# Four stages of a two-block transformer kernel: head loads, conv output, filler products in the routing, and the first expert's buffer given back in parts

## The chip, the core and the metric

The kernel runs on one core of one Trainium2 chip. The metric is the device time of one execution in microseconds (us). Engines are named as in the profile: PE (TensorE), with PEld for its weight loads, DVE (VectorE), ACT (ScalarE), POOL (GpSimd) and SP (SyncE). ACTq and SPq are the queues of ACT and SP at the place where they issue transfers.

## The reference

Two blocks follow each other on 256 tokens of 1024 features in fp32. The first has two layers, each a mixer, a SwiGLU network of 2816 columns and a gated embedding term. The second is a conformer convolution and a mixture of 32 experts, two for each token. What the change touches is the very start and the second block:

```python
h = rmsnorm(h, g_mix[0]); mix = even_mixer(h, ev_w_in, ...)       # the head
...
sh1, sc1, g1, sh2, sc2, g2 = split(silu(c) @ ada_w + ada_b, 6)
u = (rmsnorm_2(x, g) * (1 + sc1) + sh1) @ w_in + b_in
y = depthwise_conv31(a * sigmoid(gate)) + b_dw
x = x + g1 * (silu(layernorm(y, ln_g, ln_b)) @ w_out)
h = rmsnorm_2(x, norm_ffn_g) * (1 + sc2) + sh2
grp = argmax(h @ w_rg + b_rg); top 2 of the group's 8 experts by h @ w_re + b_re
x = x + g2 * sum(share * ((silu(h @ w_gate[e]) * (h @ w_up[e])) @ w_down[e]))
return rmsnorm_2(x, final_g)
```

## The kernel before

Each engine has its own written-out order, and semaphores tie the orders together. A dense product runs as three fp32r products of split operands. ACT writes the high part of a weight piece (`w_hi`, `split_hi`, L413), DVE the low part (`w_lo`, `split_lo`, L418), and PE does three passes (L444 to L446). A piece is 128x1024. Four piece buffers are in use, so a split waits until PE has used the piece four before it. SP issues nearly all loads, in one order; a wait in that order holds everything behind it.

**The head.** ACT first issues twelve small loads of parameter rows into `rows_a` (`load_rows`, L1271). Then it squares the two tiles of `h` (L903). DVE makes `rstd` from the sums (L828 to L838), ACT and DVE scale the tiles (L877, L926), PE turns them (L976). ACT makes `xT_hi` from each pair of chunks and the gain in `cols_a`, and DVE makes `xT_lo`. The first projection `ev_in` then starts at L460. PE fills its wait with small products of `ones` (`warm_up`, L487). SP issues `x`, three weight loads and then small tensors. After the load of `ev_in` 2 it issues `positions` and the two routing weights (`load_late`).

**The conv output.** DVE runs the last taps, then PE averages the channels (L2513), DVE subtracts (L2626), and PE sums the squares. DVE makes `cf_r`. PE spreads two gate rows and two columns over the partitions (`pe_rows`, `pe_eights`). Then comes a loop over eight chunks: DVE scales `xn` (`normed`), ACT applies Tanh and the shift (L2566, L2568), DVE joins them (`finish`, L2643), ACT writes `xT_hi` (L2536), and DVE writes `xT_lo` (`low`, L2648). `conv_out` 0 and 1 are the two halves of the output columns, of four pieces each. The weights of half 1 are multiplied by a gate row first (`weigh`, L2663). ACT copies the gate rows to `g_bc` (`act_rows`, L2413) and the columns to `feature_cols` (`act_eights`, L2398).

**The routing.** PE computes logits (L2721), adds the residual into four banks (L3019), waits for DVE's choice of experts (`CHOSEN`), and counts places (L2731 to L2735). DVE turns the counts into places (L2811) and the selection (L3310), on which the first gather waits (L3048). `stay_busy` (L482) and `warm_up` (L487) are products that nobody reads.

**The experts.** They run in 16 pairs. For each expert PE does gate and up (L3084), and for a pair the down product (L3122). There are three buffers for gate and up weights and four for down weights. `gu_used` counts experts whose gate and up are done, `down_used` counts pairs. SP loads expert e+3's gate and up weights after expert e's products, and down weights of two experts after the pair that held them. The first halves of the first buffers are given back earlier, through `up_used`. An expert is 2048 KB for each of gate, up and down.

## Time and profile before

| | us |
|---|---|
| median of 3 executions (lowest, highest) | 1256.05 (1254.77, 1258.88) |
| the profiled execution, its own time | 1254.8 |
| its span | 1253.1 |
| PE busy | 1216.1 |
| DVE busy | 721.4 |
| ACT busy | 519.4 |

The span is the stretch from the first to the last instruction; 1.7 us of the execution's time lie around it. The first 800 us are dense work in which the loads rest at times. The last 450 us are the experts, in which the loads move about 429 GB/s without a pause.

### The profile page before, as it was taken

How to read it: one execution, taken by the hardware profiler on the slowest of the kernel's cores; microseconds unless marked ns; L12 is line 12 of the kernel's file. 1: busy time of each engine (PE TensorE's matmuls, PEld its weight loads, DVE VectorE, ACT ScalarE, POOL GpSimd, SP SyncE). 2: the span in 40 equal slices, each digit the busy share in tenths (PEclk: the TensorE clock that was granted, in tenths of full speed). 3: DMA queues.
4: the chain of work that ended last, by engine and by line, in shares of the span. 5: the costliest groups of instructions: out<-in, count | busy, mean ns of one | idle time of the engine just before them, and what ended most of it. 6: DMA issues, size and time to landing. Idle time of an engine off the chain costs nothing.

```text
span 1253.1 us, 16148 instructions
## 1 busy us (share of the span) xinstructions
PE 1216.1 (97%) x6246; PEld 821.3 (66%) x6246; DVE 721.4 (58%) x1337; ACT 519.4 (41%) x903; POOL 48.1 (4%) x96
## 2 busy tenths in 40 slices
PE   9999999999999999999999999999999999999996
PEld 8997888887777778888877976634444334443332
DVE  5786877777758778777778988522222222222222
ACT  5554444444567654444456435422232222232222
POOL 0000000000000000000002800000000000000000
PEclk9999999999999999999999999999999999999998
DMA  8558777651631397766614486999999999999995
GB/s 294 198 217 298 269 269 268 246 190 68 228 135 31 110 364 268 269 252 239 229 57 147 149 277 261 358 421 404 427 428 431 427 429 429 428 427 431 428 426 206
DMA packets 121564, 358.07 MB, mean 286 GB/s; under 512 B 8890, under 2 KB 67955, under 8 KB 105106
## 3 DMA queue, kind: packets, MB, share of 16 engines
q1 hardware_dynamic: 114912, 331.85, 68.4%
q0 software_dynamic: 6336, 25.17, 5.1%
q8 instruction: 47, 0.77, 0.2%
q14 instruction: 27, 0.22, 0.0%
q10 hardware_dynamic: 242, 0.06, 0.0%
HBM read 352.58 MB, written 1.05 MB: 282 GB/s over the span
## 4 chain that ended last, share of the span: by engine, by line
PE 80%; DVE 7%; DMA 7%; ACT 3%; issue 1%; ACTq 0%; SPq 0%; DVEq 0%
PE ps L444 15%; PE ps L446 15%; PE ps L445 15%; PE ps L3084 14%; PE ps L3122 7%; DMA third_gate_up<-in_moe_w_up 5%; DMA second_expert<-in_moe_w_up 2%; DVE w_lo L418 2%; PE ps L3060 2%; PE ps L2503 1%; DVE xn L2600 1%; PE ps L3138 1%; PE ps L3067 1%; PE ps L3141 1%; PE ps L1039 1%
## 5 line engine op out<-in xcount | busy, mean ns | idle before, releaser
L413 ACT CAST w_hi<-dense_weights 128x1024 fp32r<-128x1024 f32 (+1 forms) x228 | 235.4, 1042 | 234.0 <-PE ps L446 194.5
L418 DVE TENSOR_TENSOR w_lo<-dense_weights,w_hi 128x1024 fp32r<-128x1024 f32 (+1 forms) x228 | 273.3, 1210 | 84.2 <-ACT w_hi L413 83.5
L444 PE MATMUL ps<-w_hi,xT_lo 128*128 128x512 f32 (+1 forms) x596 | 235.7, 395 | 4.4 <-DVE xT_lo L941 2.0
L446 PE MATMUL ps<-w_hi,xT_hi 128*128 128x512 f32 (+1 forms) x596 | 230.7, 387 | 0.0
L445 PE MATMUL ps<-w_lo,xT_hi 128*128 128x512 f32 (+1 forms) x596 | 230.3, 386 | 0.0
L444 PEld LDWEIGHTS ps<-w_hi,xT_lo 128*128 128x128 f32 x596 | 112.0, 188 | 32.0 <-issue 4.1
L446 PEld LDWEIGHTS ps<-w_hi,xT_hi 128*128 128x128 f32 x596 | 112.0, 188 | 23.3
L445 PEld LDWEIGHTS ps<-w_lo,xT_hi 128*128 128x128 f32 x596 | 112.1, 188 | 21.9 <-issue 0.2
L3268 DVE SCALAR_TENSOR_TENSOR cmask<-g_v,ps 128x256 f32<-128x256 f32 x32 | 13.5, 421 | 167.1 <-ACT g_v L3197 167.1
L3259 DVE TENSOR_TENSOR hnT<-ps,g_bc 128x512 f32<-128x512 f32 x32 | 22.1, 692 | 149.2 <-PE ps L3122 149.2
L3197 ACT ACTIVATE g_v<-ps 128x256 f32<-128x256 f32 x32 | 12.3, 384 | 206.7 <-PE ps L3084 206.7
L3084 PE MATMUL ps<-dense_weights,ge_xT 128*64 128x512 f32 x352 | 79.5, 605 | 2.9 <-DMA dense_weights<-in_moe_w_up 2.9
L3084 PE MATMUL ps<-second_expert,ge_xT 128*64 128x512 f32 x352 | 77.7, 594 | 1.4 <-DMA second_expert<-in_moe_w_up 1.4
L3084 PE MATMUL ps<-third_gate_up,ge_xT 128*64 128x512 f32 x320 | 70.7, 594 | 3.2 <-DMA third_gate_up<-in_moe_w_up 3.2
L3174 ACT ACTIVATE ge_xT<-ps,feature_cols 128x128 f32<-128x128 f32 x128 | 46.5, 467 | 65.2 <-PE ps L3067 60.3
L444 PE MATMUL ps<-w_hi,ff_hidT_lo 128*128 128x512 f32 x176 | 68.7, 390 | 0.5 <-DVE ff_hidT_lo L1144 0.5
L445 PE MATMUL ps<-w_lo,ff_hidT_hi 128*128 128x512 f32 x176 | 68.5, 389 | 0.0
L446 PE MATMUL ps<-w_hi,ff_hidT_hi 128*128 128x512 f32 x176 | 68.5, 389 | 0.0
L444 PE MATMUL ps<-xT_hi,w_lo 128*128 128x256 f32 x224 | 64.3, 287 | 3.3 <-DVE w_lo L418 2.2
L445 PE MATMUL ps<-xT_lo,w_hi 128*128 128x256 f32 x224 | 63.4, 283 | 0.0
L446 PE MATMUL ps<-xT_hi,w_hi 128*128 128x256 f32 x224 | 63.3, 283 | 0.0
L2315 DVE SCALAR_TENSOR_TENSOR ada_acc<-ada_w,c_act,ada_acc 128x512 f32<-128x512 f32 x84 | 62.6, 746 | 0.6
(441 smaller groups left out, 1844.4 us busy)
## 6 DMA issues: line engine op xcount, KB each, us to landing
ada_w<-in_ada_w POOLq DMA_DIRECT2D x12, 2048.0 KB, 12.1
dense_weights<-in_w_gate SPq DMA_DIRECT2D x22, 1024.0 KB, 7.1
dense_weights<-in_w_up SPq DMA_DIRECT2D x22, 1024.0 KB, 9.4
dense_weights<-in_w_down SPq DMA_DIRECT2D x22, 1024.0 KB, 5.1
dense_weights<-in_moe_w_gate SPq DMA_DIRECT2D x10, 2048.0 KB, 21.6
second_expert<-in_moe_w_gate SPq DMA_DIRECT2D x9, 2048.0 KB, 20.4
second_expert<-in_moe_w_up SPq DMA_DIRECT2D x9, 2048.0 KB, 24.8
third_gate_up<-in_moe_w_up SPq DMA_DIRECT2D x9, 2048.0 KB, 27.2
```

The source lines that it names most:

```text
L413: act.copy(split_view(w_hi, name, i, j), piece(name, i, j)).then_inc(hi_ready, 1)
L418: dve.tensor_tensor(split_view(w_lo, name, i, j), piece(name, i, j), split_view(w_hi, name, i, j).bitcast(F32), ALU.subtract).then_inc(pie ...
L444: pe.matmul(out, left[1], right[0], start=start, stop=False)
L445: pe.matmul(out, left[0], right[1], start=False, stop=False)
L446: return pe.matmul(out, left[0], right[0], start=False, stop=stop)
L2315: ins = dve.scalar_tensor_tensor(out=ada_acc[:], in0=w, scalar=c_col, in1=ada_acc[:], op0=ALU.mult, op1=ALU.add)
L3060: last = pe.matmul(ps[:, 2 + n, :], ge_sel_r[:, t], part[:, t, n * 512:(n + 1) * 512], start=(t == 0 and part is x_lo), stop=(t == T - 1 a ...
L3084: last = pe.matmul(out, ge_xT[:, k, e * PLACES:(e + 1) * PLACES], gate_up_rows(2 * p + e, k)[:, :, f * BLK:(f + 1) * BLK], start=(k == 0), ...
L3122: last = pe.matmul(ps[e * PLACES:(e + 1) * PLACES, n, :], ge_hidT[:, e, c, f * PLACES:(f + 1) * PLACES], down_rows(2 * p + e, 2 * f + c, n ...
L3174: act.activation(ge_xT[:, k], ps[:, 2 + k // 4, (k % 4) * P:(k % 4 + 1) * P], ACT.Identity, scale=feature_cols[:, 0, k:k + 1], bias=featur ...
L3259: dve.tensor_tensor(ge_y[:, n], ps[:, n, :], g_bc[:, 1, n * 512:(n + 1) * 512], ALU.mult).then_inc(self.gated, 1)
L3268: dve.scalar_tensor_tensor(out=ge_a, in0=ge_th[:, e], scalar=1.0, in1=ps[:, 2 + e, 0:BLK], op0=ALU.add, op1=ALU.mult).then_inc(self.half, 1)
```

## The change

The change has these parts.

1. Head: only the row `g_mix` is loaded at first. ACT loads its function table right behind it (`load_table`), and the other eleven rows are issued from ACT after six weight splits (`setup.load_rows` in `even.act`). The first weight load is cut in two. `cols_a` is filled in two steps. The fillers are 12 and 14 in place of 24 and 6. `load_late` moves behind the loads of `ev_out`. The convolution's tap rows come in two loads.
2. The first piece of a projection (`high`) is done chunk by chunk and not part by part, and waits for one chunk of `xT_hi` at a time.
3. Conv output: DVE splits `conv_out` (0, 3) before the averages. `weigh` reads the gate row in PSUM, and its first call stands in the loop at chunk 1. DVE and no longer ACT copies `feature_cols`. ACT splits `conv_out` (1, 0) before it copies the gate rows, of which it copies three and not four.
4. Loads for the first experts: expert 0's gate weights are issued after the split of `conv_out` (0, 3). Expert 1's weights go in four pairs of chunks as the pieces of `conv_out` 1 are used, and half of expert 2's up weights beside them.
5. Routing: `stay_busy(pe, 2, 1)` is gone, and the last `warm_up` has 1 product in place of 4.
6. The first expert's buffer goes back for expert 3 in three parts (after chunks 0, 1 and 3) and not in two (after 1 and 3).

```diff
@@ tokens_by_columns
-                    pe.wait_ge(*high)
-                    for part in range(2):
-                        for kk in range(2):
+                    for kk in range(2):
+                        pe.wait_ge(high[0], high[1] + kk * high[2])
+                        for part in range(2):
@@ columns, SP
-                        sp.dma_start(dst[:, 0:4], wv[:, 0:4, c:c + n]).then_inc(gu_landed[0], 16)
+                        for piece_ in range(2):
+                            cut = slice(2 * piece_, 2 * piece_ + 2)
+                            sp.dma_start(dst[:, cut], wv[:, cut, c:c + n]).then_inc(gu_landed[piece_], 16)
...
-                    elif name == "ev_in" and i == 2:
-                        setup.load_late(sp)
@@ weight_stream, behind ev_out
+            setup.load_late(sp)
             ffn(0)
@@ new helpers
+            def feature_pair(e, k):
+                cut = slice(k, k + 2)
+                for side in range(2):
+                    sp.dma_start(gate_up_of(e)[:, side, cut], (g, u)[side][:, e, cut]).then_inc(gu_landed[e % TILES], 16)
+            def split_features(e, side, pair):
+                cut = slice(2 * pair, 2 * pair + 2)
+                dst = gate_up_of(e)[:, side].rearrange("p (a b) f -> p a b f", a=2)
+                src = (g, u)[side][:, e].rearrange("p (a b) f -> p a b f", a=2)
+                sp.dma_start(dst[:, :, cut], src[:, :, cut]).then_inc(gu_landed[e % TILES], 16)
@@ loads of the first experts
             side_features(2, 0, 0, small_landed)
+            wait_split("conv_out", 0, 3, None)
+            gate_or_up(0, 0)
             sp.wait_ge(conformer.conv, KC - len(CONV_PE))
...
-            wait_split("conv_out", 0, 3, None)
-            gate_or_up(0, 0)
-            wait_split("conv_out", 1, 3, None)
-            side_features(0, 1, 1, gu_landed[0])
-            down_half(0, 0, down_landed[0])
+            for j in range(4):
+                if j == 1:
+                    wait_split("conv_out", 1, 3, None)
+                    side_features(0, 1, 1, gu_landed[0])
+                    down_half(0, 0, down_landed[0])
+                wait_used(sp, "conv_out", 1, j)
+                feature_pair(1, 2 * (PIECE_AT["conv_out", 1, j] % BUFFERS))
+                if j % 2 == 1:
+                    split_features(2, 1, j // 2)
             sp.wait_ge(h_ready, 28)
-            gate_up(1)
-            gate_or_up(2, 1)
@@ expert 3
+        FIRST_PARTS = (-1, 0, 1, KC // 2 - 1)
-                    for quarter in range(2):
-                        sp.wait_ge(up_used, 5 + quarter)
-                        cut = slice(quarter * KC // 4, (quarter + 1) * KC // 4)
+                    for part in range(3):
+                        sp.wait_ge(up_used, 5 + part)
+                        cut = slice(FIRST_PARTS[part] + 1, FIRST_PARTS[part + 1] + 1)
@@ setup
+            def load_table(self, act):
+                act.wait_ge(self.own_consts, 3)
+                act.activation(rtmp[:, 0, 0:1], ones[:, 0:1], ACT.Square)
@@ conformer, DVE
+                split_upto(dve, split_lo, "conv_out", 0, 3, ahead=0)
                 dve.wait_ge(self.conv, KC - len(CONV_PE))
...
+                    if c == 1:
+                        dve.wait_ge(mod.spread, 2)
+                        wait_a(dve, "conv_out", 1)
+                        weigh(0)
+                        mod.dve_eights(dve)
...
-                split_upto(dve, split_lo, "conv_out", 0, 3, ahead=0)
-                dve.wait_ge(mod.rows, 2)
-                wait_a(dve, "conv_out", 1)
...
-                weigh(0)
@@ conformer, ACT
-                mod.act_eights(act)
...
+                split_upto(act, split_hi, "conv_out", 1, 0, ahead=0)
                 mod.act_rows(act)
@@ routing, PE
-                stay_busy(pe, 2, 1)
                 pe.wait_ge(self.steps, self.CHOSEN)
...
-                warm_up(pe, 2, 4)
+                warm_up(pe, 2, 1)
```

ACT at the head, before: the last three row loads and what follows them.

```order
L1271 DMA rows_a<-in_od_g_qa 3x128
L1271 DMA rows_a<-in_od_g_kva 2x128
L1271 DMA rows_a<-in_ev_w_conv 12x128
L903 ACT_TABLE_LOAD
L903 ACTIVATE xn,ms<-h 128x1024 [waits h_then_stack_landed0]
L903 ACTIVATE xn,ms<-h 128x1024 [waits h_then_stack_landed1]
L413 CAST w_hi<-dense_weights 128x1024 [waits experts_gate_up_landed0]
L877 ACTIVATE xn<-h,rstd 128x1024 [waits norm_made]
```

ACT at the head in the changed kernel, from its first load:

```order
L1292 DMA rows_a<-in_g_mix 16x128
L1311 ACT_TABLE_LOAD
L1311 ACTIVATE rtmp<-ones 128x1 [waits consts_under_way]
L923 ACTIVATE xn,ms<-h 128x1024 [waits h_then_stack_landed0]
L923 ACTIVATE xn,ms<-h 128x1024 [waits h_then_stack_landed1]
L1315 COPY cols_a<-ps 128x16 [waits setup_turned]
L415 CAST w_hi<-dense_weights 128x1024 [waits experts_gate_up_landed0,columns_made]
L897 ACTIVATE xn<-h,rstd 128x1024 [waits norm_made]
L906 ACTIVATE xT_hi<-ps,cols_a 128x256 [waits norm_turned]
```

Eleven loads no longer stand ahead of the table load and the two squares; the gains' copy has moved ahead of the first split.

DVE at the start of the conv output's chunk loop, before (`cf_r` is the deviation's reciprocal, `normed` is signalled by L2652):

```order
L2652 TENSOR_TENSOR xn<-xn,cf_r 128x256 [waits cf_centred,dve_own]
L2652 TENSOR_TENSOR xn<-xn,cf_r 128x256
L2643 SCALAR_TENSOR_TENSOR mixT<-hnT,xn 128x256 [waits cf_shifted]
L2652 TENSOR_TENSOR xn<-xn,cf_r 128x256
L2643 SCALAR_TENSOR_TENSOR mixT<-hnT,xn 128x256 [waits cf_shifted]
```

The same place in the changed kernel, where the product of weights and gate row (`weigh`) and the column copy stand between:

```order
L2690 TENSOR_TENSOR xn<-xn,cf_r 128x256 [waits cf_centred,dve_own]
L2690 TENSOR_TENSOR xn<-xn,cf_r 128x256
L2686 TENSOR_TENSOR dense_weights<-dense_weights,ps 128x1024 [waits weights_a_landed1,mod_spread]
L2432 COPY feature_cols<-ps 128x16 [waits mod_spread]
L2676 SCALAR_TENSOR_TENSOR mixT<-hnT,xn 128x256 [waits cf_shifted]
```

One 128x1024 product and one small copy now stand ahead of the first `finish`.

PE in the routing from the residual on, before:

```order
L3019 MATMUL ps<-h,ident 128x512 [waits rt_steps]
L3019 MATMUL ps<-h,ident 128x512
L482 MATMUL ps<-g_v,ones 128x512
L2731 MATMUL ps<-rt,upper 128x32 [waits rt_steps]
L2732 MATMUL ps<-rt,ones 128x32
L2733 MATMUL ps<-rt,upper 128x32
L2734 MATMUL ps<-rt,ones 128x32
L2735 MATMUL ps<-rt,ones 128x32
L487 MATMUL ps<-ones 128x128 x4
L3048 MATMUL ps<-hnT,xn 128x128 [waits ge_sel_ready,rt_rows_and_exps]
```

And in the changed kernel:

```order
L3053 MATMUL ps<-h,ident 128x512 [waits rt_steps]
L3053 MATMUL ps<-h,ident 128x512
L2765 MATMUL ps<-rt,upper 128x32 [waits rt_steps]
L2766 MATMUL ps<-rt,ones 128x32
L2767 MATMUL ps<-rt,upper 128x32
L2768 MATMUL ps<-rt,ones 128x32
L2769 MATMUL ps<-rt,ones 128x32
L489 MATMUL ps<-ones 128x128
L3082 MATMUL ps<-hnT,xn 128x128 [waits ge_sel_ready,rt_rows_and_exps]
```

The 512-wide filler ahead of the counting products is gone, and one filler in place of four stands ahead of the gather.

## Rows read from the trace of the kernel before

**Rows 1.** Windows of the experts' stage: window, length, busy by engine, PEclk, DMA share, GB/s

```profile
858.00:860.00 2.00, 2.00 (x12) 0.67 (x10) 1.87 (x4) 0.72 (x1) 0.00 (x0) 1.00 0.62 197
...
870.00:1230.00 360.00, 352.46 (x1648) 144.83 (x1644) 81.63 (x213) 92.68 (x221) 0.00 (x0) 1.00 1.01 429
```

**Rows 2.** Timeline of SP: start, duration, queue, line, transfer

```profile
789.73 0.53 SPq L729 DMA_DIRECT2D g_bc<-in_moe_w_down  x1
...
857.73 0.38 SPq L736 DMA_DIRECT2D third_down<-in_moe_w_down  x1
```

**Rows 3.** Chain that ended last, first microseconds: start, duration, what

```profile
5.42 0.30 ACTq L1271
5.75 1.28 ACT L903
7.05 2.20 ACT xn L903 x4
```

**Rows 4.** Landing times of h, then of dense_weights up to 22 us

```profile
DMA to landing us min/median/max: 3.8/4.2/4.6
...
DMA to landing us min/median/max: 6.9/11.4/14.4
```

**Rows 5.** Timeline of ACT and DVE in the first projection

```profile
25.27 1.02 ACT L1438 COPY gm_v<-ps 128x1024 f32<-128x1024 f32 x1 [1.67 <-PE ps L446]
...
29.44 1.22 DVE L418 TENSOR_TENSOR w_lo<-dense_weights,w_hi 128x1024 fp32r<-128x1024 f32 x1
```

**Rows 6.** Chain, behind the first projection's last piece

```profile
36.12 0.88 PE ps L1340 x8
```

**Rows 7.** Timeline of SP, the routing weights and the loads around ev_out

```profile
21.73 5.50 SPq L1281 DMA_DIRECT2D w_route<-in_moe_w_rg  x1
27.27 4.53 SPq L1282 DMA_DIRECT2D w_route<-in_moe_w_re  x1
...
59.14 9.11 SPq L590 DMA_DIRECT2D dense_weights<-in_ev_w_out  x4
83.78 0.37 SPq L590 DMA_DIRECT2D dense_weights<-in_w_gate  x1
```

**Rows 8.** Timeline of DVE in the conv output

```profile
757.90 0.76 DVE L2652 TENSOR_TENSOR xn<-xn,cf_r 128x256 f32<-128x256 f32 x2
760.60 0.43 DVE L2643 SCALAR_TENSOR_TENSOR mixT<-hnT,xn 128x256 f32<-128x256 f32 x1 [1.94 <-ACT xn L2568]
...
770.57 1.22 DVE L418 TENSOR_TENSOR w_lo<-dense_weights,w_hi 128x1024 fp32r<-128x1024 f32 x1
```

**Rows 9.** Timeline of ACT and PE in the conv output

```profile
759.40 0.17 ACT L2398 COPY feature_cols<-ps 128x16 f32<-128x16 f32 x1 [6.83 <-PE ps L2392]
...
775.76 0.50 PE L444 MATMUL ps<-w_hi,xT_lo 128*128 128x512 f32 x1 [0.89 <-DVE w_lo L418]
```

**Rows 10.** Chain in the routing, up to the first gather

```profile
797.80 0.86 PE ps L482 x2
...
799.70 0.97 PE ps L487 x8
800.67 3.57 PE ps L3048 x32
```

**Rows 11.** Timeline of DVE in the routing

```profile
799.38 0.22 DVE L2811 TENSOR_TENSOR cmask<-ps,rt 128x64 f32<-128x64 f32 x1 [0.79 <-PE ps L2733]
799.64 0.43 DVE L3310 TENSOR_TENSOR hnT<-cols_b,cmask 128x256 f32<-128x256 f32 x1
```

**Rows 12.** Windows of the routing, columns as in Rows 1

```profile
792.00:794.00 2.00, 2.00 (x8) 1.17 (x8) 1.04 (x6) 2.00 (x2) 0.00 (x0) 0.63 0.99 426
794.00:796.00 2.00, 2.00 (x4) 0.77 (x3) 1.79 (x11) 2.00 (x3) 0.00 (x0) 0.52 1.02 434
```

**Rows 13.** Transfers between 786 and 812 us: size, median us to landing

```profile
second_expert<-in_moe_w_up SPq DMA_DIRECT2D x1, 2048.0 KB, 12.8
...
g_bc<-in_moe_w_down SPq DMA_DIRECT2D x1, 512.0 KB, 18.5
```

More of the change, by code:

```diff
@@ L877, in act @@
                     act.activation(xn[:, 0], h[:, 0], ACT.Copy, scale=rstd[:, 0, 0:1]).then_inc(self.scaled, 1)
-                if gains is not None:
+                if gains is not None and self.index:
                     gains(act)
@@ L2394, in pe_eights, with dve_eights @@
                 last.then_inc(self.spread, 1)
-            def act_eights(self, act):
-                act.wait_ge(self.spread, 3)
-                act.copy(feature_cols[:], ps[:, 2, 0:2 * KC].rearrange("p (v k) -> p v k", v=2)).then_inc(self.rows, 1)
+            def dve_eights(self, dve):
+                dve.wait_ge(self.spread, 3)
+                dve.tensor_copy(feature_cols[:], ps[:, 2, 0:2 * KC].rearrange("p (v k) -> p v k", v=2)).then_inc(self.rows, 1)
             ROW_BANKS = (0, 1, 4, 5)
@@ L2410, in act_rows @@
                 act.wait_ge(self.spread, 2)
[L2411 to L2414 removed]
+                act.copy(g_bc[:, 0, 0:512], ps[:, self.ROW_BANKS[0], :])
+                bank = self.ROW_BANKS[2]
+                act.copy(g_bc[:, 1].rearrange("p (j n) -> p j n", j=2), ps[:, bank:bank + 2, :]).then_inc(self.rows, 1)
         class ConformerStage:
@@ L3169, in copy_x @@
                     for k in range(KC):
+                        if p == 0 and k == 0:
+                            act.wait_ge(mod.rows, 2)
                         if p == 0 and k % 4 == 0:
```

70 lines of the change are left out of this document (40 added, 30 removed).

## The prediction

> **What bounds the kernel now.** I read the windows of the experts' stage first, because that stage is a third of the time, then SP's timeline to see what its loads wait for, and then the chain and the timelines of the three places that the change touches. From 870 to 1230 us the transfers run at 429 GB/s with a DMA share of 1.01 and PE is idle for 7.5 of 360 us [rows 1]. That looks like a stage bound by transfers, so the question is from when. Between 858 and 860 us the rate is only 197 GB/s, a share of 0.62 [rows 1]: the queue had run dry. SP's next load, at 857.73, is a down weight that needs the buffer of the first pair, and SP gets it when PE ends pair 1 (`down_used` 2) [rows 2]. So up to 857.7 the loads wait for PE, and from there on the end follows at a fixed distance: 1253.1 - 857.7 = 395.4 us of span, whatever was loaded before. A microsecond that PE gains ahead of 857.7 is a microsecond of the whole. A load that lands earlier gains only if PE waits for it there, and the dip says it does not.
>
> The dense stages ahead are bound by PE and the ACT and DVE steps between its products, and their loads are released by the same splits, so a shift at the head is carried through them.
>
> **The head.** ACT's twelve row loads end at 5.72; the table load takes 1.28 and the squares run from 7.05 to 9.25 [rows 3]. In the change one row load stands ahead of the table load. The row loads take 0.4 us each ((5.72 - 0.80) / 12, the first being issued at the same 0.80 as SP's first), so the table is there at 0.8 + 0.4 + 1.3 = 2.5, and the squares wait for `x` instead. Its two tiles are issued at 0.80 and 1.3 and land after 3.8 to 4.6 [rows 4], so the second is there at 5.9 at the latest, and its square ends at 5.9 + 1.1 + 0.2 = 7.2. That is 2.05 us earlier, and `rstd`, the turns and the first product follow. The first weight load lands 6.9 us after its issue at 1.73 [rows 4], at 8.6, which would now be too late for the first split at 7.4, but it is cut in two, and half of its 1024 KB is there some 1.3 us earlier (a megabyte needs 2.4 us at 429 GB/s). Waiting for one chunk of `xT_hi` instead of two lets the first four products start 0.4 us earlier, but the second piece waits for DVE's low parts as before: 0. If both tiles land at their best, 5.1, the head gives 2.8; if the weights are the last, 1.5.
>
> What is moved costs this. Eleven row loads now stand in ACT's order behind the split of the third piece of `ev_in` 1 and ahead of the copy `gm_v`. They take 11 x 0.4 = 4.4 us, in a place where ACT was idle for 1.67 [rows 5], and the split ended there at 23.6 (25.27 - 1.67). With everything 2.1 earlier, they run from 21.5 to 25.9, and `gm_v` is copied at 25.9 and not at 23.2. DVE's chain behind the copy put the low part of the next piece at 29.44, 4.2 after the copy's start [rows 5]. It now starts at 30.1 and ends at 31.3. PE comes to this last piece at 36.12 - 12 x 0.228 - 2.1 = 31.3 [rows 6]. So the stall is 0 to 0.4, and I take 0.1. If each of these loads takes as long as in the crowded part of SP's queue, the stall is far longer (a rival, below).
>
> The routing weights' loads keep SP's queue for 5.50 and 4.53 us, with `positions` 10.8. They stood between `ev_in` 2 and 3; now they stand behind the last load of `ev_out`, which is issued by 68.3 (59.14 + 9.11), and the next load is not due until 83.78 [rows 7]. 15.5 us of room hold 10.8: 0. In the old place they delayed `ev_in` 2 and 3, for which ACT waited but PE hardly did, so that is worth 0 to 0.3; I take 0.1. The split tap rows, the later gains and the transpose of 121 rows in `pe_rest` are hidden by the eleven microseconds of PE products of `ev_in` 1, at 0.1 if not. The head gives 2.1.
>
> **The conv output.** DVE has `normed` for chunk 0 at 757.90 + 0.42 = 758.3 [rows 8], but ACT starts its chunk loop at 759.47, because it first copies `feature_cols`, for which it waits until PE's column products end at 759.36 [rows 9]. The loop is then paced by ACT (0.50 + 0.49 + 0.29 = 1.28 a chunk), and DVE waits for it, 1.94 at the first `finish` [rows 8]. Without the copy ACT starts at 758.35, 1.1 earlier. DVE's new work at this place, 1.2 for `weigh` (as the 128x1024 split, 1.22 [rows 8], one operand being in PSUM) and 0.15 for the copy, runs from 758.7 to 760.05, and the first `finish` is due at 759.4 to 760.0 and needed by ACT only at 760.4 (two Tanh and two shifts after 758.35). It lies inside the wait, so the gain is 1.1. It would be 0.5 if DVE paced the loop. PE's half 0 follows ACT's loop through `xT_lo`: 1.1 earlier.
>
> Its last piece waited for the low part at 770.57 to 771.8 [rows 8], which is moved into DVE's idle time ahead of the averages: 0.1. Half 1 then waited 0.89 for its first low part [rows 9], behind the row copy on ACT, two `weigh` and a split on DVE. In the change the first `weigh` is done and the high part comes before the row copy. DVE ends the loop at 769.5, weighs piece 1 and splits piece 0 by 772.0, and PE comes at 773.5: the wait is gone, 0.9 more. The later pieces need 2.45 us of DVE for 2.74 of PE, so no new wait. Together 2.1, at least 1.3 (0.5 for the loop), at most 2.4.
>
> **The routing.** The filler of 512 columns holds PE for 0.86 from 797.80, and the four small ones for 0.97 from 799.70, and the gather starts at 800.67 [rows 10]. DVE has chosen by 797.7 and idles 0.79 for the counts; its place and selection then end at 800.07 [rows 11]. Without the first filler the counts come 0.8 earlier, DVE goes on at 798.6 at the earliest (799.38 - 0.79), and the selection ends at 799.3. One small product of 0.24 ends before that. The gather starts at 799.4 instead of 800.67: 1.3. Bounds: 0.6, where the first product alone counts, to 1.4.
>
> **Loads of the first experts.** About 10 MB are issued earlier. The last of them was issued at 789.73 and took 18.5, to 808.2, while expert 1's up weights landed 12.8 after 788.8, at 801.6, ten microseconds before PE needed them [rows 2, 13]. No PE wait stands there, and the queue runs dry at 857 all the same: 0. The earlier part of expert 3 (0.9 us for 512 KB) goes the same way. A rule of the Trainium skill stands against the pieces: the page DMA: Bandwidth & Descriptors, under Measured (HBM to SBUF), advises batches of 1 MiB or more and calls smaller ones slower per byte. By it the 512 KB pairs would land later than the 2048 KB loads did; no row here has such a pair, and with ten microseconds of room the sum stays the same.
>
> **Sum.** 2.1 + 2.1 + 1.3 = 5.5 us. Against the profiled execution's own time this is 1254.8 - 5.5 = 1249.3. That execution and the three runs have a median of 1255.4 (1254.77, 1254.8, 1256.05, 1258.88), which is 0.6 above it, so I predict 1249.9.
>
> **Rivals.**
>
> (a) The chain is not carried whole: the conv loop is paced by DVE (-0.6), the head's landings are late (-0.6), the routing gives 0.6. Gain 3.6, time 1251.8. For it: every term rests on waits below 2 us. Against it: three independent places.
>
> (b) Earlier loads count too. If the dip at 858 vanishes because the stage is bound by transfers from its start, the queue's lead adds to the gain: it would be drained at about 797 and not at 808.2, less the 5.5 of PE's own shift, about 4 more. Time 1246. Against it: the dip itself [rows 1], and expert 3's loads must wait for PE's first chunks, so the queue idles in between.
>
> (c) The clock. From 792 to 796 the granted clock is 0.63 and 0.52 of full, that is 1.2 GHz most of the time, right behind the 36-wide logits; PE lost 2 x 0.37 + 2 x 0.48 = 1.7 us there, hidden behind DVE's choice [rows 12]. Without the fillers PE has some two microseconds of 32-wide products and waits ahead of the gather, and a second drop of this length would fall on the gather and the first expert: 1.7 lost, gain 3.8, time 1251.6. The Trainium skill, TensorE: Matmul & The Clock Gate, Part 1, says that the clock falls after idleness and returns after sustained activity, which speaks for this rival; the trace agrees that it falls behind light work. Against it: the residual's 512-wide products stay, up to 797.8.
>
> (d) Slower. ACT's eleven loads fall into the time in which SP's transfers fill the rings. SP's own loads took 5.50 and 4.53 us each at such times [rows 7]. PE's stall at `ev_in` 1 grows one for one beyond 4.4 us, so at 0.9 us a load it takes all 5.5 of the gain, and at 1.5 us each the kernel is 6.6 slower than forecast, 1256.5; at 2 us each 1262. Against it: at the head the same loads took 0.4 beside SP's traffic, and they have few packets.
>
> (e) The change shifts nothing that counts, within 0.3% of before: a later wait, say for a load in the dense stages, takes it back. Time 1255.
>
> **Chances.** Forecast 0.60 (1248 to 1251.4), (a) 0.13, (b) 0.08, (c) 0.09, (d) 0.04, (e) 0.06. A difference of 0.3%, 3.8 us against the median of before, is about what a measurement can tell. The forecast and (b) lie beyond it, with about half of (a) and (c), 0.79; (e), the rest of (a) and (c) and a part of (d) are the same, 0.18; slower 0.03. For 8 in 10 I leave out (d), (e) and the outer half of (b), and take in (a) and (c) and the spread of single runs: 1246.6 to 1253.2.
>
> **What would show it.** In the changed kernel the first square starts at about 4.6 to 5 and the second ends by 7.3; the first `ev_in` product starts near 11.3. ACT issues eleven loads in 4 to 5 us and PE's wait behind them is under 0.5. PE ends `ev_in` 1 at about 34.0. In the conv output ACT's first Tanh comes about 1 us after DVE's first scaling less than before, and PE has no wait above 0.3 between the halves. The gather starts about 1.7 us after the choice. The clock row behind the gather is 1.00. The dip of the transfer rate at the end of pair 1 is still there and at least as deep, at about 852.2, and the span ends 395 us behind it. I am wrong if that distance changes, if the dip is gone, or if a shift that is there at 36 us is smaller at 700.

## The result, and the profile after

The changed kernel takes 1250.11 us, the median of 5 runs (1248.58 to 1251.33), against 1256.05 for before (1254.31 to 1258.88); the ratio is 0.995, with a 95% interval from 0.9934 to 0.9966. The forecast was 1249.9. Its profiled execution took 1251.33 us with a span of 1249.5, 3.6 less than the 1253.1 of before; why that is less than the 5.9 of the medians is taken up below.

I follow the shift by marks, the same instruction in both traces (where no fence shows one, it is the start of that instruction in PE's timeline). First ACT's timeline at the head of the changed kernel (start, duration, engine, line, operation; in brackets the idle time before and what ended it):

```profile
1.26 1.28 ACT L1311 ACT_TABLE_LOAD   x1 [1.26 <-PEq L3519]
...
4.56 1.06 ACT L923 ACTIVATE xn<-h 128x1024 f32<-128x1024 f32 x1 [1.79 <-DMA h<-in_x]
...
5.91 1.06 ACT L923 ACTIVATE xn<-h 128x1024 f32<-128x1024 f32 x1 [0.21 <-DMA h<-in_x]
...
8.19 1.05 ACT L415 CAST w_hi<-dense_weights 128x1024 fp32r<-128x1024 f32 x1 [0.58 <-DMA dense_weights<-in_ev_w_in]
9.14 1.15 ACT L897 ACTIVATE xn<-h,rstd 128x1024 f32<-128x1024 f32 x1
...
24.77 0.30 ACTq L1296 DMA_DIRECT2D rows_a<-in_ev_w_conv  x1
25.11 1.02 ACT L1472 COPY gm_v<-ps 128x1024 f32<-128x1024 f32 x1 [3.14 <-issue]
```

The table is loaded by 2.54, the squares wait for `x` and the second ends at 7.06, where 7.2 was forecast [rows 3 for before]. The eleven row loads run from 20.93 to 25.07, 0.38 each. Then PE, up to the end of `ev_in` 1 (the turns of `ws_rows` follow it, as in rows 6):

```profile
7.33 3.39 PE L489 MATMUL ps<-ones 128*128 128x128 f32 x28
10.56 1.91 PE L996 MATMUL ps<-ident,xn 128*128 128x128 f32 x16
12.23 0.70 PE L462 MATMUL ps<-w_lo,xT_hi 128*128 128x512 f32 x2
...
34.33 1.03 PE L1371 MATMUL ps<-ident,ws_rows 128*128 128x128 f32 x8
```

The first product comes at 12.23 and not 11.3. The wait that the moved row loads could have made, in front of PE's last weight piece at 31.60, is not there, so they cost nothing. Before, the same marks stood at 13.80 and 35.95, 1.6 later. In the conv output (DVE, ACT and PE; against rows 8 and 9):

```profile
756.88 0.60 ACT L2598 ACTIVATE hnT<-xn,half 128x256 f32<-128x256 f32 x1 [5.79 <-DVE xn L2690]
...
757.09 1.22 DVE L2686 TENSOR_TENSOR dense_weights<-dense_weights,ps 128x1024 f32<-128x1024 f32 x1
758.23 0.17 DVE L2432 COPY feature_cols<-ps 128x16 f32<-128x16 f32 x1
758.31 0.42 DVE L2676 SCALAR_TENSOR_TENSOR mixT<-hnT,xn 128x256 f32<-128x256 f32 x1
...
763.77 0.47 PE L446 MATMUL ps<-w_hi,xT_lo 128*128 128x512 f32 x1 [1.05 <-DVE xT_lo L2681]
```

ACT's loop starts at 756.88, right behind DVE's first scaling, and the wait of 0.89 between the halves is gone: 763.77 is PE's last one up to 795. In the routing (against rows 10 and 11):

```profile
788.58 5.38 PE L3053 MATMUL ps<-h,ident 128*128 128x512 f32 x8
793.80 0.30 PE L2765 MATMUL ps<-rt,upper 128*128 128x32 f32 x2
...
794.83 0.47 PE L489 MATMUL ps<-ones 128*128 128x128 f32 x2
795.52 3.81 PE L3082 MATMUL ps<-hnT,xn 128*128 128x128 f32 x32 [0.22 <-DVE hnT L3346]
```

Last the mark from which I counted the end, SP's down load at the end of pair 1, and the windows around it (columns as in rows 1):

```profile
852.81 0.38 SPq L751 DMA_DIRECT2D third_down<-in_moe_w_down  x1
```

```profile
852.00:854.00 2.00, 2.00 (x12) 0.69 (x10) 1.19 (x2) 1.19 (x3) 0.00 (x0) 1.00 1.03 377
854.00:856.00 2.00, 2.00 (x12) 0.61 (x10) 1.57 (x6) 0.27 (x1) 0.00 (x0) 1.00 0.82 287
...
870.00:1230.00 360.00, 352.10 (x1639) 144.33 (x1639) 81.66 (x213) 92.71 (x222) 0.00 (x0) 0.99 1.01 427
```

The mark stands 4.92 earlier than in rows 2. The dip behind it is still there, though shallower (287 GB/s against 197), where the forecast had it at least as deep. Behind it the transfers run without a pause again. From the mark to the end of the span it is 396.7 us and not 395.4. The forecast named a change of this distance as a sign of being wrong, so I followed it further. PE's last wait for a load comes near 1191 us. These are its products behind that wait, in PE's timeline of before, of the changed kernel and of fill_both (an experiment below), in this order:

```profile
1196.29 7.09 PE L3084 MATMUL ps<-third_gate_up,ge_xT 128*64 128x512 f32 x32 [0.75 <-DMA third_gate_up<-in_moe_w_up]
1191.05 8.78 PE L3118 MATMUL ps<-third_gate_up,ge_xT 128*64 128x512 f32 x32 [2.23 <-DMA third_gate_up<-in_moe_w_up]
1192.62 7.09 PE L3119 MATMUL ps<-third_gate_up,ge_xT 128*64 128x512 f32 x32 [2.24 <-DMA third_gate_up<-in_moe_w_up]
```

In all fourteen profiles of this document these products start 338.0 to 339.1 us behind the mark, and the span ends 49.3 to 50.1 behind their end. What differs is the products themselves: 7.09 us in seven profiles and 8.78 in the other seven. In the seven longer ones the granted clock falls to the 1.2 GHz level at this place for 3.4 us. The distance to the end is 396.3 to 397.6 in these and 394.7 to 395.6 in the rest. So 1.7 us of it is the clock of that execution. Such falls earlier in the experts, near 1026 and 1164, are absorbed: fill_both had neither and a distance of 395.6, loads_old had both and 395.2. Before ran without this fall and the changed kernel with it, which is why their spans differ by only 3.6. PE's wait ahead of a fall was 2.2 to 2.3 us; two profiles had such a wait without a fall (fill_both and first_whole), and behind the waits of 0.8 to 1.2 none came.

### The profile page after: what moved, and what is told of

Its sections match the earlier page's. It is cut to its first block, busy times and chain, and to the rows that moved or that the text cites. A ratio compares the mean times of both kernels' runs of the same rounds, so it can differ in the third digit from the quotient of the medians.

```text
span 1249.5 us, 16133 instructions
## 1 busy us (share of the span) xinstructions
PE 1215.0 (97%) x6231; PEld 819.9 (66%) x6231; DVE 721.1 (58%) x1338; ACT 519.0 (42%) x904; POOL 48.0 (4%) x96
## 3 DMA queue, kind: packets, MB, share of 16 engines
HBM read 352.58 MB, written 1.05 MB: 283 GB/s over the span
## 4 chain that ended last, share of the span: by engine, by line
PE 84%; DVE 8%; DMA 5%; ACT 2%; issue 1%; SPq 0%; POOL 0%; DVEq 0%; POOLq 0%; ACTq 0%
PE ps L3118 16%; PE ps L446 15%; PE ps L448 15%; PE ps L447 15%; PE ps L3156 8%; DMA third_gate_up<-in_moe_w_up 5%; PE ps L3094 2%; DVE w_lo L420 2%; PE ps L2536 1%; PE ps L3172 1%; DVE xn L2633 1%; PE ps L3101 1%; PE ps L3175 1%; PE ps L489 1%; PE ps L1059 1%
## 5 line engine op out<-in xcount | busy, mean ns | idle before, releaser
L3118 PE MATMUL ps<-third_gate_up,ge_xT 128*64 128x512 f32 x320 | 74.0, 617 | 4.6 <-DMA third_gate_up<-in_moe_w_up 4.6
```

Source lines behind the costliest of these rows:

```text
L3118: last = pe.matmul(out, ge_xT[:, k, e * PLACES:(e + 1) * PLACES], gate_up_rows(2 * p + e, k)[:, :, f * BLK:(f + 1) * BLK], start=(k == 0), ...
```

## The experiments

Edits smaller than 2 us don't show in times that spread by 3 or 4, so every kernel was profiled, and the verdicts are read from marks. Each mark comes from one profile of its kernel. Unless said otherwise each is the changed kernel with one edit.

| kernel | first product | quads' end to conv output's end | clock at 1.2 GHz in the routing, us | residual to gather | down load of pair 1 | from there to the end | time, median |
|---|---|---|---|---|---|---|---|
| before | 13.80 | 41.26 | 3.4 | 8.07 | 857.73 | 395.4 | 1256.05 |
| before_again | 13.75 | 41.25 | 0 | 7.36 | 857.55 | 397.0 | 1254.84 |
| changed | 12.23 | 38.88 | 3.4 | 6.94 | 852.81 | 396.7 | 1250.11 |
| fill_wide | 11.78 | 38.86 | 0 | 6.84 | 852.25 | 395.2 | 1251.29 |
| fill_four | 12.42 | 38.89 | 0 | 7.13 | 852.69 | 394.7 | 1250.10 |
| fill_both | 12.36 | 38.89 | 3.4 | 8.07 | 853.74 | 395.6 | 1250.13 |
| loads_old | 11.58 | 38.89 | 6.8 | 7.84 | 853.78 | 395.2 | 1250.00 |
| xn_first | 12.36 | 38.88 | 3.4 | 6.92 | 852.70 | 396.7 | 1251.08 |
| first_whole | 12.33 | 38.89 | 0 | 6.84 | 852.63 | 395.6 | 1251.17 |
| rows_double | 12.22 | 38.87 | 3.4 | 6.93 | 859.43 | 396.7 | 1256.28 |
| eights_act | 12.49 | 40.01 | 6.8 | 8.10 | 855.86 | 397.6 | 1252.20 |
| half_old | 11.92 | 38.89 | 6.8 | 7.84 | 854.19 | 394.8 | 1250.79 |
| turn_fillers | 11.66 | 38.90 | 0 | 6.84 | 852.18 | 397.4 | 1250.26 |
| best | 12.21 | 38.90 | 3.4 | 7.10 | 852.87 | 396.3 | 1250.89 |

The quads end where the averages' products of 128x256 start (744.05 in the changed kernel), the conv output where the turns of `h` start (782.93). The fourth column is twice the sum of what each 1 us window between 784 and 800 lacks of a granted clock of 1.00, since the lower level is half.

### before_again

The kernel before without an edit.

> The kernel before, unchanged, profiled a second time: how far its marks move by themselves. Theory (the gain is in the program's order): first product at 13.8 within 0.4, end of the first projection at 36, 41.3 us from the end of the quads to the end of the conv output, 8.1 us from the residual to the gather unless the clock falls for longer, and the down load of pair 1 at 857.7 within 1 us with the end 395.4 us behind it, within 1. Rival (the first profile was an unlucky one): marks more than 1 us earlier, so that a part of the 4.9 us between the two traces is no effect of the change.

The marks repeat: 13.75, 41.25, and 857.55 for the down load. The gather comes 7.36 behind the residual and not 8.07, as the clock did not fall this time. The first profile was no unlucky one. The distance to the end moved by 1.6 with nothing edited: this execution had the fall behind the last wait, the first one had not.

### rows_double

```diff
-                    act.dma_start(dst, src).then_inc(self.rows_landed, 16)
+                    for cut in (slice(0, P // 2), slice(P // 2, P)):
+                        act.dma_start(dst[:, cut], src[:, cut]).then_inc(self.rows_landed, 16)
```

> The changed kernel with each of ACT's eleven row loads issued as two of half the columns: 22 issues in the place where there were 11, the same bytes. Theory (each issue holds ACT for 0.37 as in the changed kernel, where the eleven took 4.1 and left 1.2 us between the last low part at 30.51 and PE's need of it at 31.7): ACT copies gm_v 4.1 later, PE waits 4.1 - 1.2 = 2.9 for the last piece of the second half of the projection, its end moves from 34.33 to about 37.2, and the time is 2.9 us more. Rival (the next loads are late anyway, so a wait there is given back): the end moves, but less than 1 us of it is left at the conv output. If an issue took longer in the crowd, as the slower rival of the forecast had it, the wait would be longer than 2.9.

ACT's timeline, then PE's, of this kernel:

```profile
29.78 0.72 ACTq L1297 DMA_DIRECT2D rows_a<-in_ev_w_conv  x2
30.54 1.01 ACT L1473 COPY gm_v<-ps 128x1024 f32<-128x1024 f32 x1 [8.57 <-issue]
```

```profile
36.00 0.80 PE L446 MATMUL ps<-w_hi,xT_lo 128*128 128x512 f32 x1 [4.24 <-DVE w_lo L420]
36.59 0.63 PE L447 MATMUL ps<-w_lo,xT_hi 128*128 128x512 f32 x1
...
41.22 1.04 PE L1372 MATMUL ps<-ident,ws_rows 128*128 128x128 f32 x8
```

```profile
36.00:41.00 5.00, 5.00 (x12) 3.94 (x13) 3.35 (x3) 0.00 (x0) 0.00 (x0) 0.50 0.80 266
```

The 22 issues took 9.6 us, 0.44 each and not 0.37, so `gm_v` is copied 5.43 later. About 1.0 of that is room, and PE's first product on the last piece starts 4.40 later (36.00 instead of 31.60; the row shows 4.24 of it as idle). What neither theory had is that PE then comes back at a granted clock of 0.50, the 1.2 GHz level: its twelve products take 0.43 each instead of 0.23, 2.5 us more. The projection ends 6.9 later, the down load of pair 1 comes 6.6 later, and the time is 1256.28, that of before (ratio 1.0003, 0.9993 to 1.0014). The rival falls: a delay at 36 us is carried over 820 us. The Trainium skill, TensorE: Matmul & The Clock Gate, Part 1, has the clock fall after idleness; by that rule this is to be expected, and the row agrees.

### turn_fillers

```diff
-                warm_up(pe, 3, 14)
+                warm_up(pe, 3, 10)
```

> The changed kernel with ten fillers in place of fourteen ahead of the first turns. In the changed kernel they run from 7.33 to 10.7, while ACT has scaled its tile by 10.3, and the first turn starts at 10.56. Four fewer end 0.97 earlier. Theory (the fillers, which the forecast did not count, held back the turns in the slower of the two ways in which they run; where they run fast, as in two of the runs so far, they end at 9.9 and don't matter): the turns start when ACT's scaling ends, at 9.8 to 10.3, and the first product at 11.6 to 12.0. Rival (the scaling alone sets it, or the clock falls in the gap): first product still at 12.2 or later, or a granted clock under 1.00 behind 10 us.

```profile
7.47 2.50 PE L489 MATMUL ps<-ones 128*128 128x128 f32 x20
9.94 1.97 PE L996 MATMUL ps<-ident,xn 128*128 128x128 f32 x16
11.66 0.71 PE L462 MATMUL ps<-w_lo,xT_hi 128*128 128x512 f32 x2
```

ACT's scaling ends at 9.88 (8.74 + 1.14), the turns start at 9.94, and the clock stays at 1.00. The first product is 0.57 earlier than in the changed kernel, but not all of this is the fillers: here the first split started at 7.79 and not at 8.19. In the changed kernel ACT's scaling ended at 10.29 and the turns started at 10.56, so the fillers alone held them by 0.2 there, and the late split by the rest. Against fill_four, whose split also started at 7.79 and whose turns came at 10.76, the turns are 0.8 earlier. So the fillers ahead of the turns, which the change raised from 6 to 14, take 0.2 to 0.8 from the head, by how early the weights land.

### first_whole

```diff
-                        for piece_ in range(2):
-                            cut = slice(2 * piece_, 2 * piece_ + 2)
-                            sp.dma_start(dst[:, cut], wv[:, cut, c:c + n]).then_inc(gu_landed[piece_], 16)
+                        sp.dma_start(dst[:, 0:4], wv[:, 0:4, c:c + n]).then_inc(gu_landed[0], 16)
```

> The changed kernel with the first 1024 KB of weights as one transfer, not two. Theory (the landing is set by its bytes, half of them 1.3 us earlier): the split starts at 9.5 instead of 8.2, ACT's scaling behind it at 10.5, and the first product at 13.5 to 13.6 instead of 12.23; the end of the first projection moves as much, 34.33 to about 35.6, and the time is 1.3 us more. Rival (the latency of a transfer decides and not its size): less than 0.5 later.

```profile
8.46 1.05 ACT L415 CAST w_hi<-dense_weights 128x1024 fp32r<-128x1024 f32 x1 [1.42 <-DMA dense_weights<-in_ev_w_in]
...
10.61 1.97 PE L994 MATMUL ps<-ident,xn 128*128 128x128 f32 x16 [0.67 <-ACT xn L895]
```

Against the changed kernel the rival holds. The whole 1024 KB are there at 8.46; the half came at 8.19 in the changed kernel and at 7.41 to 8.24 in the four others in which ACT waited for it. The first product at 12.33 is 0.1 later than in the changed kernel. The turns do wait for ACT here (0.67), as the fillers happened to end early. Halving this transfer brought its landing forward by 0.2 to 1.1, not by the 1.3 that I had counted, and the first product by 0.1 in these two executions. That 0.1 flatters the whole transfer, since the changed kernel's fillers ended late. Against the three profiles whose fillers ended as early as here (11.78, 11.58 and 11.92 in fill_wide, loads_old and half_old) the first product is 0.4 to 0.75 later, which is more than the rival allows in two of them and less than the theory's 1.3 in all.

### xn_first

ACT's scaling of the first tile is written ahead of its first split.

> The changed kernel with ACT's scaling of the first tile ahead of the split of the first weight piece (in the changed kernel the split stands ahead, starts when the piece lands at 8.19 and ends at 9.24, while rstd is ready at 8.64). Theory (part of the head's gain is lost since the weights' piece lands later than was forecast and ACT scales behind its split): the turns start 0.4 to 0.5 earlier, but the low part of the first piece is then ready at 12.0 only, and the first product reads it, so that starts 0.2 earlier, at about 12.0 where the piece lands at 8.2. Rival (the turns are what the first product waits for): the whole 0.5, 11.7. The time changes by less than a run's spread either way.

Neither holds: the scaling starts at 8.89 and ends at 10.04, and yet the turns start at 10.69, where the fillers end, and the first product at 12.36. This is what led to turn_fillers (above).

### eights_act

```diff
-                        mod.dve_eights(dve)
...
+                mod.act_eights(act)
                 for c in range(KC):
                     act.wait_ge(self.normed, c + 1)
```

> The changed kernel with the copy of feature_cols on ACT again, ahead of its chunk loop. In the changed kernel the loop starts at 756.88, while PE's column products end at 757.88. Theory (the loop is paced by ACT, so its start sets PE's half 0): ACT copies at 757.9 and starts the loop at 758.0, 1.1 later, and the way from the end of the quads to the end of the conv output is 40.0 instead of 38.88. Rival (DVE's product of the gate, which stands in the loop, already holds it): less than 0.5.

```profile
758.17 0.17 ACT L2432 COPY feature_cols<-ps 128x16 f32<-128x16 f32 x1 [6.83 <-PE ps L2426]
```

40.01 instead of 38.88: the copy's place is worth 1.13, where 1.1 was forecast. Most of the rest of this kernel's delay at the down load is the clock in the routing, 1.67 (see loads_old).

### half_old

```diff
-                split_upto(act, split_hi, "conv_out", 1, 0, ahead=0)
                 mod.act_rows(act)
...
-                        dve.wait_ge(mod.spread, 2)
-                        wait_a(dve, "conv_out", 1)
-                        weigh(0)
...
+                dve.wait_ge(mod.spread, 2)
+                wait_a(dve, "conv_out", 1)
+                weigh(0)
                 for j in range(4):
```

> The changed kernel with half 1 handed over as before: ACT copies the rows ahead of the first high part, and DVE weighs the first piece behind its loop; but it still reads the gate row from PSUM, so that it doesn't wait for ACT's row copy. The forecast gave 0.9 for the whole of this (wait of 0.89 in rows 9). Theory (what cost the 0.89 was DVE's wait for ACT's two row copies): with the gate in PSUM the first piece is weighed by 769.2, its high part made by ACT at 770.2, and its low part by 771.5, before PE comes at 772.0: the way from the quads to the end stays 38.9, within 0.15. Rival (the order of the splits cost it): the wait is back, 39.5 or more.

```profile
766.80 0.98 DVE L2680 TENSOR_TENSOR xT_lo<-mixT,xT_hi 128x256 fp32r<-128x256 f32 x2
767.70 2.34 DVE L2685 TENSOR_TENSOR dense_weights<-dense_weights,ps 128x1024 f32<-128x1024 f32 x2
770.10 1.22 DVE L420 TENSOR_TENSOR w_lo<-dense_weights,w_hi 128x1024 fp32r<-128x1024 f32 x1
```

38.89, no wait between the halves. The early `weigh` and the split ahead of the row copy are worth nothing as long as the other edits stand; with those, the low part is ready at 771.3 and PE comes at 771.7 (782.65, its end, less 48 products of 0.228). This kernel has two things that before had not: the gate row is read from PSUM, and the split of `conv_out` (0, 3) is done ahead of the averages. The theory credits the first alone, which isn't shown. In DVE's timeline of before the two `weigh` start like this:

```profile
772.06 2.36 DVE L2663 TENSOR_TENSOR dense_weights<-dense_weights,g_bc 128x1024 f32<-128x1024 f32 x2 [0.27 <-ACT g_bc L2413]
```

DVE waited only 0.27 for ACT's row copy, because the split of (0, 3) had kept it until 771.79 (rows 8). So I estimate from these rows that reading PSUM alone would have saved 0.3 of the 0.89, and that the moved split was needed for the rest. No kernel has one without the other.

### fill_wide, fill_four, fill_both

```diff
+                stay_busy(pe, 2, 1)
                 pe.wait_ge(self.steps, self.CHOSEN)
...
-                warm_up(pe, 2, 1)
+                warm_up(pe, 2, 4)
```

The first hunk is fill_wide, the second fill_four.

> The changed kernel with the 512-wide filler put back behind the residual, and nothing else. In the changed kernel the counting products start at 793.80 and the gather at 795.52. Theory (the filler delays the counts, and DVE waits for them): the counts start 0.8 later, at 794.6, the gather at 796.3, and the down load at the end of pair 1 (852.81) at 853.6. Rival (PE is not what the gather waits for, DVE's choice is): the counts wait for DVE anyway and the gather moves by less than 0.2. Granted clock between 794 and 800 stays 1.00 under both; a lower one in the changed kernel than here would have spoken for the clock rival, and it is 1.00 there already.

> The changed kernel with four small fillers ahead of the gather in place of one. One ends 0.24 behind the other, so they end at 795.8 instead of 795.1. Theory (now DVE's selection, which ends at 795.37, is last): the gather moves from 795.52 to 795.8, 0.3 us, since 0.4 of the 0.7 lie in the wait for DVE. Rival (PE's order alone decides, as if the fillers were all on the path): 0.7 us, 796.2. End of pair 1 at 853.1 or 853.5.

> The changed kernel with both kinds of filler as before the change. Theory: gather at 796.7 to 796.8, 1.2 to 1.3 later than 795.52, and the end of pair 1 as much later, 854.0 to 854.1; the time 1.2 us more. Rival (the two savings hide each other): 0.8, as with the wide one alone.

fill_wide misses: the gather is 6.84 behind the residual, as early as in any kernel. PE in this kernel, and DVE's choice:

```profile
790.25 1.99 PE L3054 MATMUL ps<-h,ident 128*128 128x512 f32 x4 [0.18 <-DVE rts L2829]
792.07 1.02 PE L484 MATMUL ps<-g_v,ones 128*128 128x512 f32 x2
793.13 0.41 PE L2766 MATMUL ps<-rt,upper 128*128 128x32 f32 x2
...
792.85 0.23 DVE L2836 TENSOR_TENSOR rt<-rt 128x64 f32<-128x64 f32 x1
```

Here the clock did not fall. The residual is done at 792.1, and the filler lies wholly ahead of the choice at 793.08. In fill_both the clock was at 1.2 GHz for 3.4 us, the residual ended with the choice, and the two fillers cost 1.13 (8.07 against 6.94 and 6.92, at the same fall). fill_four, without a fall, costs 0.29, as its theory had it (0.3). fill_both stays a little under its theory: 1.13 instead of 1.2 to 1.3, with the down load 0.93 later, and its time shows nothing. So the wide filler costs nothing when the clock does not fall ahead of it, and 0.8 when it does; the 0.8 is the 1.13 less fill_four's 0.29, since fill_wide itself had no fall. In all of these the clock behind the choice was 1.00.

### loads_old

```diff
-            wait_split("conv_out", 0, 3, None)
-            gate_or_up(0, 0)
             sp.wait_ge(conformer.conv, KC - len(CONV_PE))
...
+            wait_split("conv_out", 0, 3, None)
+            gate_or_up(0, 0)
+            wait_split("conv_out", 1, 3, None)
+            side_features(0, 1, 1, gu_landed[0])
+            down_half(0, 0, down_landed[0])
             sp.wait_ge(h_ready, 28)
+            gate_up(1)
+            gate_or_up(2, 1)
```

> The changed kernel with the loads of experts 0 to 2 issued where they were before the change, the three-part give-back kept. Theory (early landings are worth nothing, the queue runs dry at the end of pair 1 either way): the down load at the end of pair 1 is issued at 852.8 within 0.2, the last early load lands at about 804 and not near 798, and the time agrees with the changed kernel within 1 us. Rival (the experts' stage is bound by transfers from its start): the dip behind 852 goes, and the time is 3 to 4 us more, 1253 to 1254.

The down load comes at 853.78, 0.97 later, outside what the theory allowed; PE's marks tell why:

```profile
784.41 4.44 PE L2752 MATMUL ps<-w_route,hnT 128*128 128x36 f32 x32
788.65 6.28 PE L3049 MATMUL ps<-h,ident 128*128 128x512 f32 x8
794.77 0.30 PE L2761 MATMUL ps<-rt,upper 128*128 128x32 f32 x2
```

```profile
788.00:792.00 4.00, 4.00 (x8) 2.14 (x9) 2.73 (x16) 3.92 (x6) 0.00 (x0) 0.50 1.05 451
792.00:796.00 4.00, 4.00 (x17) 2.28 (x15) 2.42 (x14) 0.20 (x1) 0.00 (x0) 0.76 0.98 418
```

The clock was down for 6.8 us. That cost 0.75 in the logits and 0.90 in the residual and what follows, 1.65 in all, less the 0.69 by which this execution was ahead at the quads. From the gather to the down load it is 57.29, as in the changed kernel (57.29) and in before (57.23). The dip is there (172 GB/s from 854 to 856 us), and the time is that of the changed kernel. The early loads are worth nothing that the mark or the time can tell, and the rival falls. half_old and eights_act had the same long fall at the cost of 1.66 and 1.67. Three profiles of fourteen had the long fall. Whether their edits had a part in it isn't shown, since each kernel but before was profiled once.

### best

Ten fillers ahead of the turns, the first piece of weights issued by ACT, and one residual product behind the counts. The piece is read from other columns of `ev_w_in` (0 to 511 and not 2048 to 2559), so the values differ from the reference's; sizes and order are the same.

> Three edits of the changed kernel: ten fillers ahead of the turns; the first 512 KB piece of weights issued by ACT behind its first row load (at 1.26, instead of 1.73 by SP); and the residual of tile 0, second half, moved from ahead of the choice to behind the counts, in place of the last filler. Theory: the piece lands at about 7.7, so that its split ends by 8.7 and the first product starts at 11.5 to 11.7 instead of 12.23; in the routing a clock drop no longer holds the counts back (in the changed kernel the residual ended 0.25 behind the choice, in the one with the old loads 1.1), so the counts start 4.9 to 5.0 behind the residual's start and the gather 6.8 to 6.9; together 0.6 to 0.8 us less than the changed kernel, too little for the times to tell. Rival (the moved product ends behind DVE's selection, or the added issue delays the table and the squares): one of the two marks later than in the changed kernel by 0.3 or more.

```profile
1.26 0.44 ACTq L3423 DMA_DIRECT2D dense_weights<-in_ev_w_in  x1
...
6.52 1.06 ACT L924 ACTIVATE xn<-h 128x1024 f32<-128x1024 f32 x1 [0.71 <-DMA h<-in_x]
...
8.00 1.04 ACT L415 CAST w_hi<-dense_weights 128x1024 fp32r<-128x1024 f32 x1 [0.27 <-DMA dense_weights<-in_ev_w_in]
```

```profile
794.71 1.10 PE L3053 MATMUL ps<-h,ident 128*128 128x512 f32 x2
795.65 1.61 PE L3082 MATMUL ps<-hnT,xn 128*128 128x128 f32 x13
```

It is no better. With the earlier transfer of weights `x`'s second tile lands 0.6 later (the square starts at 6.52), and the weights land at 8.00, 0.2 earlier and not 0.5. Together this eats the gain of the fewer fillers; and the moved product holds the gather, at 7.10, though the counts start at 5.02, about as expected. No version here beats the changed kernel by more than the times can tell; turn_fillers has the earliest down load, 852.18, and a time of 1250.26.

## Why the prediction was right

**The frame.** The end follows the down load of pair 1 by a nearly fixed distance, and what is gained ahead of it counts one for one: shown. Over fourteen profiles the mark moved by 7.3 us and the distance stayed between 394.7 and 397.6. The distance did change between the two kernels, by 1.3, which I had named as a sign of being wrong. Its cause, as far as fourteen profiles go, is not the change but the fall of the clock behind PE's last wait for a load: before_again, with that fall and nothing edited, has 397.0. So the frame needs one correction: behind that last wait, near 1191 us, PE sets the pace again, and 1.7 us lost there are lost whole.

**The time.** The sum was 0.6 too large at the mark (4.92, or 4.74 against before_again, where I forecast 5.5). The medians differ by 5.94, with an interval from 4.3 to 8.3 by the ratio's, which holds both. The 63 later executions of before have a median of 1255.54, from which the changed kernel's gain is 5.4. Their spread goes with the clock: 1257.4 to 1258.9 in the eleven whose mean granted clock was 0.990 or 0.991, and 1253.3 to 1256.6 in the 43 with 0.994 or more. The agreement within 0.2 us is partly luck: the head and the routing gave less than forecast, the conv output more, and the medians moved by more than the marks.

**The head: 2.1 forecast, 1.6 measured.** The squares, the table and `rstd` came as worked out: `rstd` is ready at 8.64 and was at 10.81, 2.2 earlier. The step that fell short is "`rstd`, the turns and the first product follow". Between `rstd` and the turns 0.7 was lost: ACT scaled its tile behind a split that began only with the landing at 8.19, which cost 0.5, and PE then stood in its own fillers until 10.56, which cost 0.2. The landing of "half of its 1024 KB some 1.3 us earlier" was too hopeful, at 0.2 to 1.1 by first_whole. Over the eight profiles with the changed kernel's order at the head the first product came at 11.58 to 12.49, a gain of 1.3 to 2.2. Of the 1.6, 1.5 is left at the end of the quads (744.05 against 745.52), and more against the second profile of before (746.07). The moved row loads cost nothing, with about 1.0 us of room where I had a stall of 0 to 0.4.

**The conv output: 2.1 forecast, 2.4 measured** (41.26 to 38.88). The 1.1 of the copy is shown (1.13). The 0.9 between the halves is right in size, but "the first `weigh` is done and the high part comes before the row copy" is not its cause: half_old has neither and no wait. What is left as the cause is the gate row read from PSUM together with the moved split of (0, 3), not told apart. The remaining 0.4 no kernel isolates. The traces point to the finer waits for single chunks, which I put at 0: PE's first product comes 2.51 behind the start of ACT's loop (759.39 - 756.88) where it came 3.80 behind it (763.27 - 759.47). PE then waits 1.05 for a low part, so that 0.3 is left of the 1.3 at the end of half 0.

**The routing: 1.3 forecast, 1.1 measured** (8.07 to 6.94), and 0.5 where the clock does not fall (7.36 to 6.84). The first 0.8 hangs on the clock: my row of before happened to have a fall, and so had the changed kernel, which is luck. Of the 0.5, 0.29 is the three small fillers. The other 0.2 lies ahead of the second half of the residual (a wait of 0.41 in before_again against 0.18 in fill_four) and was not taken apart.

**The loads of the first experts: 0**, shown by loads_old. The Trainium skill's rule on small transfers (DMA: Bandwidth & Descriptors, Measured), which spoke against the pieces, would change little: from 786 to 798 us the changed kernel moved 420 GB/s and loads_old 429, so the trace agrees in direction, but PE waited for none of it. The give-back of the first buffer in three parts was not tried alone. The traces show no gain from it: the way from the gather to the mark is 57.23 in before and 57.29 in the changed kernel, and from the mark to PE's last wait for a load it is 338.6 and 338.2. The moves of `load_late` and of the tap rows were not tried alone either.

**The rivals.** (b) fell with loads_old; its "about 4 more" is 5.7 by its own figures (808.2 - 797 - 5.5). (c) did not come behind the removed fillers, where the clock was 1.00 in every profile. But the fall ahead of them, which I called hidden, is hidden only in part: of the long one, 6.8 us, 1.7 lie on the path, and with the short one PE is as late as DVE's choice or a little later. (d) is real as a mechanism, and its first price holds: "at 0.9 us a load it takes all 5.5 of the gain", and rows_double, with 0.87 for each row, ends at the time of before. The mark came 6.6 later there, where the rule gives 9.6 - 4.4 = 5.2: I had left out 2.5 at the slow clock behind the wait and, the other way, the room of 1.0. Its other prices are wrongly added. By its own rule 1.5 us a load is 16.5 - 4.4 = 12.1 above the forecast, 1262, and 2 us is 1267.5; that rows_double's 1256.28 lies near the 1256.5 named for 1.5 us means nothing. (a), a gain of less than the sum because one term is late, is what the marks show in part; (e) did not happen.

## What to carry to other kernels

Find the last place where the transfers wait for the engines and the last place where an engine waits for a transfer. Gains count ahead of the first and behind the second, and between the two they are mostly absorbed. Then follow one instruction per stage through both traces, since a sum of terms of 1 to 2 us can't be read from times that spread by 4. Fillers that keep a clock up are instructions like others: when the chain ahead of them gets shorter, they are next in line, and whether one lies on the path can depend on the clock of that execution. A wait of PE can cost more than the wait: the one of 4.24 us brought 2.5 us at the lower clock, and the waits of 2.2 us late in the experts brought 1.7 in seven profiles of nine.

## What the runs showed of the hardware

- In the routing the granted clock fell to the 1.2 GHz level in 9 of 14 profiles, always in the 36-wide products of the logits or within 0.5 us of their end, for 3.4 us (six times) or 6.8 us (three times), and in 5 not at all, with the same program order ahead of it. What stands ahead is 2.2 us of turns of `h` and 3.5 to 4.3 us of these narrow products; no run tells the two apart. PE's rows show it as busy there, so this is not plain idleness, which is what the rule of the Trainium skill (TensorE: Matmul & The Clock Gate, Part 1) speaks of.
- The 24 products that the twelve fillers at the kernel's start make took 4.55 to 4.83 us in four profiles of the changed order and 5.40 to 5.49 in the other eight, which moves the turns behind them by up to 0.9.
- Behind PE's last wait for a load the granted clock fell for 3.4 us in 7 of 14 profiles, which made 32 products take 8.78 us and not 7.09. The wait was 2.2 to 2.3 us in these seven and in two without a fall, and 0.8 to 1.2 in the other five.
- At the head 512 KB landed 5.7 to 6.5 us after the issue at 1.73 (five profiles), and 1024 KB after 6.7 in first_whole and 6.9 in before.
- A DMA issue held ACT for 0.38 us among eleven and 0.44 among 22 of half the size.
